# Reordered stage ends, joined score matmuls and narrow value matmuls in a two-layer decoder trunk

## The chip, the cores and the metric

The kernel runs on one core of a Trainium2 chip. The metric is the device time of one execution in microseconds (us), median over runs. A core has a matrix engine (PE, whose weight loads are shown as PEld), a vector engine (DVE), an activation engine (ACT), a general engine (POOL) and a queue that starts transfers (SP). They run side by side and wait for one another on semaphores; each works through its own instructions in the order in which they are written.

## What is computed

Two layers over 512 tokens of 1024 features. Layer 0 mixes tokens by differential attention, layer 1 by native sparse attention (NSA); both go on with a gated MLP and a gated per-layer embedding:

```python
hn = rms_norm(x, g0); a = mixer(hn); x = x + rms_norm(a, g1)
hn = rms_norm(x, g2); f = conv_ffn(hn); x = x + rms_norm(f, g3)
gate = sigmoid(rms_norm(x, ple_g) @ gate_w); x = x + gate * (p[i] @ proj_w)
# differential attention, 8 heads: two score maps, their softmaxes p0 and p1
a = p[:, :, 0] - lam * p[:, :, 1]; o = a @ v; o = rms_norm(o, subln_g); out = o @ w_out
# NSA, 4 groups of 4 heads: three branches, gated
s_c = q @ k_cmp; p_c = masked_softmax(s_c); o_c = p_c @ v_cmp   # compressed keys and values
o = o_c * gates[..., 0] + o_s * gates[..., 1] + o_w * gates[..., 2]; out = o @ w_out
```

With 512 tokens the selected and the window branch both see every earlier key.

## The kernel before

All projections read their weights as *units* of 128x1024 numbers, in one fixed order (PLAN). SP loads a unit into one of four raw buffers, ACT copies it as the high part w_hi (`w_high`), and POOL forms the low part w_lo in four pieces (`low`). PE multiplies three times for each product: high by high, high by low, low by high. `weights(u)` on PE waits until the low parts of all units before u are done. Activations are split in the same way: PE transposes a tile, ACT copies it as nT_hi, DVE subtracts and writes nT_lo. Eight PSUM banks are named A[0..3] and B[0..3]. The order of the work on each engine is written by hand, as one long program an engine.

*Start.* For each of four token tiles: statistics (ACT), xn (DVE), transposes (PE), nT_hi, nT_lo, then the matmuls of the first two units v on that tile.

*Differential heads.* `head(h, ...)` takes four query tiles qt in turn: scores in B, maxima (DVE), two exponentials (ACT), the mix (DVE, amix), transposes into A[2] (`turn_mix`), their copy pT (ACT, `p_turned`), values into A[3]. The head before is normalised at the same time: ACT squares, DVE sums, POOL takes the inverse root by Newton steps and writes o_nrm, PE turns it into A[2] (`turn_o`), ACT and DVE split it (`oT_high`, `oT_low`). The last head has no next head's projections to fill PE; it has parts of the output projection (`early`, units 24 to 26) instead. The output projection's first unit is 27 (PLAN["out0"]).

*Embedding step.* `embed` ends layer 0; its last tile overlaps with the norms for layer 1, in which ACT switches between sigmoid and root.

*NSA groups.* `group(g, first)` projects two query units, the keys and the values, ropes them (DVE), makes the compressed scores (L1651), then takes 16 steps (h, k), in which k stands for query tile ORDER[k] = 0, 3, 1, 2 and n = (tile + 1) * 128 keys. A step has two branches c: scores in B[2 * (k % 2) + c], maxima, two exponentials into gp, transposes into A[2] and A[3] (`gturn`), copies gpT (ACT for c = 0, DVE for c = 1), and values into A[c] (`gvalues`). PE's order in the loop is gturn(n), scores(n+2), values(n-1). Before the loop stand the turning of the compressed weights pc (`cturn`, into A[3], copied as pcT), the turning of the values (`vturn`, into A[0], copied as Vg), and the compressed values (`cvalues(0)`, `cvalues(1)`, read by DVE's `blocks_out`).

The matmul of the values reads 128 columns though only 64 of them are read later:

```python
m = pe.matmul(A[c][:, tok(qt)], gpT[:, k % 2, c, kb * P:(kb + 1) * P],
              Vg[:, kb, HEAD * c:HEAD * c + P], start=kb == 0, stop=kb == qt)
```

## Time and profile before

| | before |
|---|---|
| median of 3 runs | 1501.54 us (1501.36 to 1501.85) |
| profiled execution | 1501.17 us, span 1499.4 us |
| PE busy, share of the span | 97% |
| PE weight loads | 81% |
| DVE, ACT, POOL | 48%, 48%, 46% |
| mean granted clock of PE | 0.998 |
| moved by DMA | 127.80 MB, 85 GB/s |

The span goes from the first to the last instruction. In a timeline row the first number is the start, the second the length of the instruction or of the merged run (xN instructions of one kind). A length of a matmul includes its way through the array, so matmuls start more closely than their lengths say. A bracket shows how long the engine stood idle before the row and what released it. fp32r operands make one matmul record, plain f32 operands two.

### The profile page before, as it was taken

What the parts mean: (1) busy time and instruction counts of PE and PEld (TensorE: products, weight loads), DVE (VectorE), ACT (ScalarE), POOL (GpSimd) and SP (SyncE); (2) the same over time, 40 slices, a digit from 0 to 9 for tenths busy, and PEclk for the clock granted to TensorE, in tenths of its full rate; (3) what the DMA queues carried; (4) which work ended last, traced back from release to release, by engine and by line L of the source; (5) the groups of instructions that cost most, each with busy time, mean ns of one, the idle gap of its engine ahead of it and who ended that gap; (6) DMA issues with size and microseconds to landing.
All of it is one profiled execution on the core that took longest, in us unless ns stands there. A gap on an engine that the chain in (4) does not pass through costs nothing.

```text
span 1499.4 us, 23490 instructions
## 1 busy us (share of the span) xinstructions
PE 1461.4 (97%) x7566; PEld 1215.3 (81%) x7566; DVE 722.3 (48%) x1257; ACT 713.4 (48%) x1298; POOL 688.3 (46%) x982
## 2 busy tenths in 40 slices
PE   6999999999999999999999999999999999999998
PEld 5877768888888888878878888888888888888887
DVE  5477773643434300345476767673544443410053
ACT  5245555644444413456464646464554444423262
POOL 4634446665655655363420211112466565655452
PEclk9999999999999999999999999999999999999999
DMA  6321113323232322242310101001232323232221
GB/s 212 115 71 57 56 43 113 118 97 107 84 100 96 100 96 98 69 159 95 128 57 16 43 15 42 28 28 37 87 116 98 98 87 107 86 111 93 92 98 57
DMA packets 38139, 127.80 MB, mean 85 GB/s; under 512 B 6208, under 2 KB 6976, under 8 KB 37824
## 3 DMA queue, kind: packets, MB, share of 16 engines
q1 hardware_dynamic: 32832, 117.46, 23.4%
q10 hardware_dynamic: 5248, 9.55, 1.8%
q8 instruction: 37, 0.61, 0.2%
q14 instruction: 22, 0.18, 0.0%
HBM read 124.90 MB, written 2.10 MB: 85 GB/s over the span
## 4 chain that ended last, share of the span: by engine, by line
PE 40%; issue 34%; POOL 21%; DVE 2%; ACT 2%; POOLq 0%; ACTq 0%; DVEq 0%
POOL w_lo L304 21%; PE banks_a L1282 21%; PE banks_a L1292 8%; PE banks_b L1292 7%; PE banks_b L1466 1%; PE banks_a L1485 1%; PE banks_a L1255 1%; PE banks_b L1469 0%; ACT y L371 0%; ACT w_hi L368 0%; PE banks_b L1255 0%; DVE nm L1004 0%; DVE xn L832 0%; ACT pT L625 0%; DVE amix L1017 0%
## 5 line engine op out<-in xcount | busy, mean ns | idle before, releaser
L304 POOL TENSOR_TENSOR w_lo<-w_raw,w_hi 128x256 fp32r<-128x256 f32 x864 | 658.7, 795 | 750.6 <-ACT w_hi L368 750.3
L368 ACT ACTIVATE w_hi<-w_raw 128x1024 fp32r<-128x1024 f32 x216 | 228.9, 1062 | 267.9 <-PE banks_b L1292 115.0
L1282 PE MATMUL banks_a<-nT_hi,w_hi 128*128 128x512 f32 (+1 forms) x968 | 344.3, 377 | 0.0
L1282 PE MATMUL banks_a<-nT_lo,w_hi 128*128 128x512 f32 (+1 forms) x968 | 343.2, 376 | 0.7 <-DVE nT_lo L838 0.7
L1282 PE MATMUL banks_a<-nT_hi,w_lo 128*128 128x512 f32 (+1 forms) x968 | 342.1, 375 | 1.1 <-POOL w_lo L304 1.0
L1282 PEld LDWEIGHTS banks_a<-nT_hi,w_lo 128*128 128x128 f32 x968 | 173.5, 189 | 33.8 <-POOL w_lo L304 1.5
L1282 PEld LDWEIGHTS banks_a<-nT_lo,w_hi 128*128 128x128 f32 x968 | 173.8, 189 | 31.9 <-DVE nT_lo L838 0.9
L1282 PEld LDWEIGHTS banks_a<-nT_hi,w_hi 128*128 128x128 f32 x968 | 173.7, 189 | 31.9 <-ACT nT_hi L401 0.3
L910 DVE SCALAR_TENSOR_TENSOR y<-banks_a,conv,y 128x511 f32<-128x511 f32 x88 | 66.0, 750 | 217.7 <-ACT y L494 217.2
L494 ACT ACTIVATE y<-banks_a,conv 128x512 f32<-128x512 f32 x88 | 68.6, 780 | 206.6 <-PE banks_a L1282 206.5
L1004 DVE TENSOR_REDUCE nm<-banks_b 128x2 f32<-128x256 f32 (+2 forms) x96 | 79.2, 825 | 22.6 <-PE banks_b L1469 10.3
L741 ACT ACTIVATE gp<-banks_b,nm 128x128 f32<-128x128 f32 (+3 forms) x128 | 67.6, 528 | 44.4 <-DVE nm L1004 38.7
L1719 PE MATMUL banks_a<-Vg,gpT 128*128 128x128 f32 x640 | 84.6, 280 | 0.0
L1719 PEld LDWEIGHTS banks_a<-Vg,gpT 128*128 128x128 f32 x640 | 76.5, 192 | 0.3
L849 DVE TENSOR_TENSOR y<-banks_b,g_post 128x512 f32<-128x512 f32 x16 | 11.1, 692 | 131.9 <-ACT y L371 131.9
L912 DVE SCALAR_TENSOR_TENSOR y<-banks_a,conv,y 128x510 f32<-128x510 f32 x88 | 65.9, 749 | 12.1
L1292 PE MATMUL banks_a<-w_hi,hT_hi 128*128 128x512 f32 x176 | 69.1, 392 | 0.0
L1292 PE MATMUL banks_a<-w_hi,hT_lo 128*128 128x512 f32 x176 | 68.5, 389 | 0.0
L1292 PE MATMUL banks_a<-w_lo,hT_hi 128*128 128x512 f32 x176 | 68.5, 389 | 0.0
L1292 PE MATMUL banks_b<-w_hi,hT_hi 128*128 128x512 f32 x176 | 68.5, 389 | 0.0
L1292 PE MATMUL banks_b<-w_lo,hT_hi 128*128 128x512 f32 x176 | 68.5, 389 | 0.0
L1292 PE MATMUL banks_b<-w_hi,hT_lo 128*128 128x512 f32 x176 | 68.5, 389 | 0.0
(262 smaller groups left out, 2386.8 us busy)
## 6 DMA issues: line engine op xcount, KB each, us to landing
w_raw<-in_w SPq DMA_DIRECT2D x216, 512.0 KB, 3.3
g_pre<-in_gains ACTq DMA_DIRECT2D x6, 512.0 KB, 4.6
x<-in_x SPq DMA_DIRECT2D x4, 512.0 KB, 8.4
g_post<-in_gains ACTq DMA_DIRECT2D x4, 512.0 KB, 5.7
out<-x SPq DMA_DIRECT2D x8, 256.0 KB, 2.0
pe_raw<-in_pT ACTq DMA_DIRECT2D x2, 512.0 KB, 6.0
w1k<-in_w ACTq DMA_DIRECT2D x1, 1024.0 KB, 5.7
w1v<-in_w ACTq DMA_DIRECT2D x1, 1024.0 KB, 7.8
```

The source lines that it names most:

```text
L304: pool.tensor_tensor(w_lo[slot][:, cols], w_raw[k % RAW][:, cols], w_hi[slot][:, cols].bitcast(F32), ALU.subtract).then_inc(S["w_lo_done"], 1)
L368: act.activation(w_hi[u % RING][:, :], w_raw[u % RAW][:, :], ACT.Copy).then_inc(S["w_hi_done"], 1)
L494: signal(act.activation(dst, bank[:, :], ACT.Identity, bias=conv[:, bass.ds(4 * f + 3, 1)], scale=conv[:, bass.ds(4 * f + 2, 1)]), "aff_do ...
L741: signal(act.activation(gp[:, k % 2, c, 0:n], B[2 * (k % 2) + c][:, 0:n], ACT.Exp, bias=nm[:, qt, c:c + 1], accum_out=sums[:, h % 2, qt, c ...
L910: link(dve.scalar_tensor_tensor(dst[:, 1:SEQ], bank[:, 0:SEQ - 1], conv[:, bass.ds(4 * f + 1, 1)], dst[:, 1:SEQ], ALU.mult, ALU.add))
L912: last = dve.scalar_tensor_tensor(dst[:, 2:SEQ], bank[:, 0:SEQ - 2], conv[:, bass.ds(4 * f, 1)], dst[:, 2:SEQ], ALU.mult, ALU.add)
L1004: signal(dve.tensor_reduce(nm[:, qt, :], banks_b[:, b:b + 2, 0:n], AX.X, ALU.max, negate=True), negmax, step + 1)
L1255: return pe.matmul(dst, src, ident[:, :], start=True, stop=True, is_transpose=True)
L1282: m = pe.matmul(bank[:, cols], w[:, k * P:(k + 1) * P], r[:, k, cols], start=(k, pas) == (0, 0), stop=(k, pas) == (KT - 1, 2))
L1292: m = pe.matmul(bank[:, :], a[:, kk, tok(t)], w[:, c * HALF:(c + 1) * HALF], start=(kk, pas) == (first, 0), stop=(kk, pas) == (last, 2))
L1466: pe.matmul(B[2 * (qt % 2) + c][:, 0:n], qT[p][rows, tok(qt)], kT[p][rows, 0:n], start=True, stop=False)
L1719: m = pe.matmul(A[c][:, tok(qt)], gpT[:, k % 2, c, kb * P:(kb + 1) * P], Vg[:, kb, HEAD * c:HEAD * c + P], start=kb == 0, stop=kb == qt)
```

## The change

1. Start: PE waits for unit v+1's low part before its second unit and not before its first; on ACT the copies of units 2 and 3 stand ahead of nT_hi of tiles 2 and 3.
2. Last differential head: the early part of tile 1, unit 26, moves ahead of turn_mix(2); unit 27's matmuls on tile 0 (`first_output`) fill the places behind the turnings; turn_o of head 6 goes to B[1]; values(2) comes before turn_mix(3).
3. Embedding step: the copy of unit Ub+5 stands ahead of the last sigmoid.
4. Group 0: the subtraction for kc's low part and a memset move ahead of DVE's work on the first queries; the exp table is asked for earlier.
5. All groups: cturn goes to A[1]; the first exponentials stand ahead of the copy pcT; one Vg copy and not two; the second exponentials stand ahead of the first gpT copy; both compressed values come behind the first turning; DVE takes the second maxima ahead of the compressed sums.
6. Scores of both branches lie in one bank for n <= 256 and are made by joined matmuls.
7. Value matmuls read 64 columns.

```diff
--- before.py
+++ after.py
@@ -203,7 +203,7 @@
             ("cm", [P, 2, TT * N_PAD], F32),
-            ("Vg", [P, TT, P + HEAD], F32), ("vT", [P, SEQ], F32),
+            ("Vg", [P, TT, P], F32), ("vT", [P, SEQ], F32),
@@ -248,6 +248,17 @@
             return cols.rearrange("p (n j o) -> p o j n", j=CMP_STRIDE // 2, o=2)[:, odd, :, :]
+        def score_columns(k):
+            n, b = (ORDER[k] + 1) * P, 2 * (k % 2)
+            if n <= 2 * P:
+                return banks_b[:, b, 0:2 * n].rearrange("p (c n) -> p c n", c=2)
+            return banks_b[:, b:b + 2, 0:n]
+        def turned_o(h):
+            return B[1] if isinstance(h, int) and h == DIFF_HEADS - 2 else A[2]
@@ -556,9 +567,9 @@
                 link(square(x[:, 2, HALF:D], ss[:, 1, 2:3], y0[:, 2, :]))
+                w_high(Ub + 5)
                 second(3)
                 root(q, 2)
-                w_high(Ub + 5)
                 stats(q, 3)
@@ -578,10 +589,10 @@
             input_stats(3)
+            w_high(2)
+            w_high(3)
             nT_high(0, 2)
             nT_high(0, 3)
-            w_high(2)
-            w_high(3)
             act.wait_ge(S["consts_ready"], 5)
...
@@ -773,23 +784,23 @@
                            8 * g + 6 + c + 1)
+                if first:
+                    act.activation(std[:, TT:TT + 1], eps[:, :], ACT.Exp)
                 act.wait_ge(S["cexp_in"], g + 1)
                 signal(act.activation(vT[:, :], A[2], ACT.Copy), "vT_done", g + 1)
+                gexps(*seq[0])
                 act.wait_ge(S["cpT_done"], g + 1)
-                signal(act.activation(pcT[:, :, :], A[3].rearrange("p (t n) -> p t n", t=TT), ACT.Copy),
+                signal(act.activation(pcT[:, :, :], A[1].rearrange("p (t n) -> p t n", t=TT), ACT.Copy),
                        "cpTc_done", g + 1)
-                gexps(*seq[0])
                 act.wait_ge(S["vTt_done"], g + 1)
                 v3 = A[0].rearrange("p (t n) -> p t n", t=TT)
-                link(act.activation(Vg[:, :, 0:P], v3, ACT.Copy))
-                signal(act.activation(Vg[:, :, P:P + HEAD], v3[:, :, 0:HEAD], ACT.Copy), "vg_done", g + 1)
+                signal(act.activation(Vg[:, :, :], v3, ACT.Copy), "vg_done", g + 1)
+                gexps(*seq[1])
                 for n, (h, k) in enumerate(seq):
                     gp_turned(h, k)
-                    if n == 0:
-                        gexps(*seq[1])
                     if n == 3:
@@ -797,7 +808,7 @@
             group(0, True, u=UG)
-            with chain.loop(1, GROUPS, 1) as g:
+            with chain.loop(1, GROUPS, 0) as g:
                 group(g, False, i=g, u=UG, per=4)
@@ -997,12 +1008,13 @@
-            def maxima(qt, b, scores, negmax, step):
+            def maxima(qt, b, scores, negmax, step, columns=None):
                 dve.wait_ge(S[scores], 2 * step + 2)
-                signal(dve.tensor_reduce(nm[:, qt, :], banks_b[:, b:b + 2, 0:n], AX.X, ALU.max, negate=True), negmax,
-                       step + 1)
+                if columns is None:
+                    columns = banks_b[:, b:b + 2, 0:n]
+                signal(dve.tensor_reduce(nm[:, qt, :], columns, AX.X, ALU.max, negate=True), negmax, step + 1)
...
@@ -1155,6 +1167,11 @@
                             goT_low(2 * g - 2 + m, m)
+                    if n == 0 and first:
+                        dve.wait_ge(S["kchi_done"], 1)
+                        dve.tensor_tensor(kc[:, :, 1, :], kcmp[:, :, :], kc[:, :, 0, :].bitcast(F32), ALU.subtract)\
+                            .then_inc(S["kclo_done"], 1)
+                        dve.memset(Kl[side(1), :, :].bitcast(F32), 0.0)
                     if n < 2:
@@ -1163,10 +1180,6 @@
                     if n == 1 and first:
-                        dve.wait_ge(S["kchi_done"], 1)
-                        dve.memset(Kl[side(1), :, :].bitcast(F32), 0.0)
-                        dve.tensor_tensor(kc[:, :, 1, :], kcmp[:, :, :], kc[:, :, 0, :].bitcast(F32), ALU.subtract)\
-                            .then_inc(S["kclo_done"], 1)
                         dve.wait_ge(S["cm_in"], 16)
@@ -1195,6 +1208,7 @@
                     .then_inc(S["cp_done"], 1)
+                gmaxima(*seq[1])
                 dve.wait_ge(S["cp_done"], g + 1)
...
@@ -1217,9 +1230,10 @@
-                blocks_out(0)
                 for n, (h, k) in enumerate(seq):
                     gp_turned(h, k)
+                    if n == 0:
+                        blocks_out(0)
                     if n + 2 < len(seq):
@@ -1428,9 +1442,9 @@
                     pe.wait_ge(S["nlo_done"], 2 * t)
-                    if t == 1:
-                        weights(PLAN["v"] + 2)
                     for n in range(2):
+                        if t == 1:
+                            weights(PLAN["v"] + n + 1)
                         m = of_tiles(PLAN["v"], n, (t - 1,), A, nT_hi, nT_lo, KT)
@@ -1489,7 +1503,7 @@
                 for t in range(TT):
-                    m = transpose(A[2][:, tok(t)], o_nrm[:, t, :])
+                    m = transpose(turned_o(h)[:, tok(t)], o_nrm[:, t, :])
                 m.then_inc(S["oT_done"], 1)
@@ -1523,8 +1537,10 @@
                         early(0, *(n for n in parts if n < 2))
-                    elif parts[0]:
-                        early(1, 2)
+                def first_output(c):
+                    weights(PLAN["out0"] + 1)
+                    tokens(B[0], PLAN["out0"] % RING, c, oT0_hi, oT0_lo, c, 0, KT)
                 pe.wait_ge(S["qrope_done"], h + 1)
@@ -1539,7 +1555,17 @@
                     later_part(h + 2, p, 0, 4)
+                if not keys:
+                    early(1, 2)
                 turn_mix(h, 2)
+                if not keys:
+                    first_output(0)
+                    turn_o(h - 1)
+                    values(h, 2)
+                    turn_mix(h, 3)
+                    first_output(1)
+                    values(h, 3)
+                    return
                 later_queries(0)
@@ -1570,7 +1596,9 @@
             U = PLAN["out0"]
-            by_unit(U, range(3), B, oT0_hi, oT0_lo, KT, last_head)
+            pe.wait_ge(S["oTlo_done"], DIFF_HEADS - 1)
+            of_tiles(U, 0, (1, 2, 3), B, oT0_hi, oT0_lo, KT).then_inc(S["units_done"], 1)
+            by_unit(U, range(1, 3), B, oT0_hi, oT0_lo, KT, last_head)
             last_of_first(U, 3, B, oT0_hi, oT0_lo, KT, last_head)
@@ -1657,7 +1685,7 @@
                     for t in range(TT):
-                        m = transpose(A[3][:, tok(t)], pc[:, t, :, :].rearrange("p h n -> p (h n)"))
+                        m = transpose(A[1][:, tok(t)], pc[:, t, :, :].rearrange("p h n -> p (h n)"))
                     m.then_inc(S["cpT_done"], 1)
@@ -1685,13 +1713,21 @@
                         pe.wait_ge(S["gprobs_done"], 2 * step(h, k) - 2)
+                    both = score_columns(k)
+                    if n <= 2 * P:
+                        for K in (Kh, Kl):
+                            pe.matmul(both, Q[h][:, tok(qt)], K[:, :, 0:n], start=K is Kh, stop=False)
+                        pe.matmul(both[:, :, n - P:n], ident_b[:, :],
+                                  causal_b[:, :].unsqueeze(1).broadcast_to([P, 2, P]), start=False,
+                                  stop=True).then_inc(S["gscores_done"], 2)
+                        return
                     for c in range(2):
                         for K in (Kh, Kl):
-                            pe.matmul(B[2 * (k % 2) + c][:, 0:n], Q[h][:, tok(qt)], K[:, c, 0:n],
-                                      start=K is Kh, stop=False)
+                            pe.matmul(both[:, c, :], Q[h][:, tok(qt)], K[:, c, 0:n], start=K is Kh, stop=False)
                     for c in range(2):
-                        pe.matmul(B[2 * (k % 2) + c][:, n - P:n], ident_b[:, :], causal_b[:, :], start=False,
+                        pe.matmul(both[:, c, n - P:n], ident_b[:, :], causal_b[:, :], start=False,
                                   stop=True).then_inc(S["gscores_done"], 1)
@@ -1716,8 +1752,8 @@
                         for kb in range(qt + 1):
-                            m = pe.matmul(A[c][:, tok(qt)], gpT[:, k % 2, c, kb * P:(kb + 1) * P],
-                                          Vg[:, kb, HEAD * c:HEAD * c + P], start=kb == 0, stop=kb == qt)
+                            m = pe.matmul(A[c][:, qt * P:qt * P + HEAD], gpT[:, k % 2, c, kb * P:(kb + 1) * P],
+                                          Vg[:, kb, side(c)], start=kb == 0, stop=kb == qt)
                     m.then_inc(S["gpv_done"], 1)
@@ -1743,7 +1779,6 @@
                 vturn()
-                cvalues(0)
                 for n, (h, k) in enumerate(seq):
@@ -1751,6 +1786,7 @@
                     else:
+                        cvalues(0)
                         cvalues(1)
```

## Rows read from the trace of the kernel before

**Rows 1.** Page of the profile, first part: busy time, share, instructions.

```profile
PE 1461.4 (97%) x7566; PEld 1215.3 (81%) x7566; DVE 722.3 (48%) x1257; ACT 713.4 (48%) x1298; POOL 688.3 (46%) x982
```

**Rows 2.** Who waited for whom, PE: total us, times, longest us.

```profile
PE banks_a L1255 <- ACT gp L741: 3.9, 4, 1.0
```

**Rows 3.** Timeline at the start: start us, us, instruction, [idle before it <- releaser].

```profile
13.49 1.40 DVE L838 TENSOR_TENSOR nT_lo<-banks_a,nT_hi 128x512 fp32r<-128x512 f32 x2
...
17.02 0.76 PE L1292 MATMUL banks_a<-w_hi,nT_hi 128*128 128x512 f32 x1 [2.28 <-POOL w_lo L304]
...
21.64 1.04 PE L1255 MATMUL banks_b<-ident,xn 128*128 128x128 f32 x8
...
22.33 1.23 ACT L401 ACTIVATE nT_hi<-banks_b 128x512 fp32r<-128x512 f32 x2 [4.63 <-PE banks_b L1255]
```

**Rows 4.** Busy time by stretch, and the granted clock (after POOL's figures).

```profile
225.00:229.00 4.00, 3.79 (x14) 3.13 (x15) 1.48 (x2) 0.85 (x2) 0.00 (x0) 0.59 0.00 0
...
757.50:761.50 4.00, 4.00 (x14) 3.21 (x14) 3.83 (x8) 2.10 (x4) 0.92 (x2) 0.58 0.37 131
```

**Rows 5.** Timeline of the last differential head and of its output projection.

```profile
224.03 0.55 PE L1255 MATMUL banks_a<-ident,amix 128*128 128x128 f32 x3 [1.19 <-DVE amix L1017]
225.21 0.71 PE L1255 MATMUL banks_a<-ident,o_nrm 128*128 128x128 f32 x4 [0.63 <-ACT pT L625]
...
230.93 0.47 PE L1292 MATMUL banks_b<-w_hi,oT_hi 128*128 128x512 f32 x1
...
241.95 0.60 PE L1255 MATMUL banks_a<-ident,o_nrm 128*128 128x128 f32 x4
...
230.00 2.01 ACT L368 ACTIVATE w_hi<-w_raw 128x1024 fp32r<-128x1024 f32 x2
...
240.49 1.04 POOL L333 TENSOR_TENSOR o_nrm<-o_raw,osum 128x512 f32<-128x512 f32 x1
```

**Rows 6.** Timeline of the change from layer 0's embedding step to layer 1.

```profile
695.79 0.60 ACT L526 ACTIVATE sg<-banks_b 128x512 f32<-128x512 f32 x1 [1.05 <-issue]
...
698.02 1.06 ACT L368 ACTIVATE w_hi<-w_raw 128x1024 fp32r<-128x1024 f32 x1
...
703.35 1.22 PE L1282 MATMUL banks_a<-nT_hi,w_lo 128*128 128x256 f32 x8 [1.00 <-POOL w_lo L304]
```

**Rows 7.** Timeline of the entry into group 0.

```profile
747.85 1.42 DVE L1162 TENSOR_TENSOR Q<-banks_b,Q 64x512 fp32r<-64x512 f32 x2 [2.73 <-ACT Q L758]
...
754.54 0.91 DVE L1167 MEMSET Kl<- 64x1024 f32 x1 [0.27 <-DVE Q L1162]
...
755.90 1.94 PE L1651 MATMUL banks_a<-kc,Q 128*128 128x64 f32 x16 [1.66 <-DVE kc L1168]
...
764.07 1.28 ACT L777 ACT_TABLE_LOAD   x1 [2.23 <-DVE sc L1190]
...
766.84 0.66 PE L1255 MATMUL banks_a<-ident,pc 128*128 128x128 f32 x4 [0.18 <-DVE pc L1196]
```

**Rows 8.** Timeline of the first turnings of group 2.

```profile
909.64 0.66 PE L1255 MATMUL banks_a<-ident,pc 128*128 128x128 f32 x4
...
915.48 1.09 PE L1255 MATMUL banks_a<-ident,gp 128*128 128x128 f32 x8 [1.04 <-ACT gp L741]
```

**Rows 9.** Timeline of PE's small matmuls in group 2.

```profile
918.11 0.30 PE L1691 MATMUL banks_b<-Kh,Q 128*128 128x128 f32 x1
...
918.72 2.00 PE L1719 MATMUL banks_a<-Vg,gpT 128*128 128x128 f32 x16
920.56 0.82 PE L1255 MATMUL banks_a<-ident,gp 128*128 128x128 f32 x6
...
923.35 0.36 PE L1691 MATMUL banks_b<-Kh,Q 128*128 128x256 f32 x1
923.55 0.28 PE L1691 MATMUL banks_b<-Kl,Q 128*128 128x256 f32 x1
...
900.27 1.97 PE L1651 MATMUL banks_a<-kc,Q 128*128 x16
```

More of the change, by code:

```diff
@@ L637, in oT_high @@
                 act.wait_ge(S["oT_done"], h + 1)
-                signal(act.activation(oT0_hi[:, bass.ds(h, 1), :].rearrange("p a n -> p (a n)"), A[2][:, :],
+                signal(act.activation(oT0_hi[:, bass.ds(h, 1), :].rearrange("p a n -> p (a n)"), turned_o(h),
                                       ACT.Identity, scale=subg[:, :]), "oThi_done", h + 1)
@@ L740, in gexps @@
                             act.wait_ge(S["gT_done"], 2 * step(h, k) - 2)
-                        signal(act.activation(gp[:, k % 2, c, 0:n], B[2 * (k % 2) + c][:, 0:n], ACT.Exp,
+                        signal(act.activation(gp[:, k % 2, c, 0:n], score_columns(k)[:, c, :], ACT.Exp,
                                               bias=nm[:, qt, c:c + 1],
@@ L1037, in oT_low @@
                 signal(dve.scalar_tensor_tensor(
-                    oT0_lo[:, bass.ds(h, 1), :].rearrange("p a n -> p (a n)"), A[2][:, :], subg[:, :],
+                    oT0_lo[:, bass.ds(h, 1), :].rearrange("p a n -> p (a n)"), turned_o(h), subg[:, :],
                     oT0_hi[:, bass.ds(h, 1), :].rearrange("p a n -> p (a n)").bitcast(F32), ALU.mult, ALU.subtract),
@@ L1122, in gmaxima @@
                 def gmaxima(h, k):
-                    maxima(ORDER[k], 2 * (k % 2), "gscores_done", "gnegmax_done", step(h, k))
+                    maxima(ORDER[k], 2 * (k % 2), "gscores_done", "gnegmax_done", step(h, k), score_columns(k))
                 def gp_turned(h, k):
```

1 line of the change is left out of this document (removed).

## The prediction, made before the changed kernel was run

> **What bounds the kernel now.** I read the page of the profile first, then who waited for whom, then the timeline at each place the diff touches, then the busy time by stretch. The page says that one engine sets the time: PE is busy for 97% of the span, the others for under half [rows 1]. So only two things can gain: PE work that goes away, and places where PE stands still. In the waits, note how small they are: the largest repeated one is 3.9 us in four pieces of at most 1.0 [rows 2]. The rest sit at the ends of stages, each with its releaser: 2.28 us at the start [rows 3], 1.19 and 0.63 in the last differential head [rows 5], 1.00 before layer 1 [rows 6], 1.66 at the entry of group 0 [rows 7], and about 1 in each group [rows 8]. Two of these cost more than their length: right behind them the granted clock is 0.59 and 0.58 for 4 us, that is, half of it at the 1.2 GHz level [rows 4], some 1.6 us lost each time, for a pause of under 2 us.
>
> **The change part by part.** The sum is made against the profiled execution's own 1501.17 us (span 1499.4); the median of the three runs is 1501.54, so 0.4 more.
>
> *Start.* PE waited for the low parts of units 0 and 1; now only unit 0's hold back the first matmul, and what comes last is nT_lo, done at 13.49 + 1.40 = 14.89 [rows 3]. The first matmul moves from 17.02 to 15.0: gain 2.0. Unit 1's low parts are done before PE has finished its six matmuls of unit 0, since they were ready at 17.0. The twelve matmuls of the first tile took 21.64 - 17.02 = 4.62 us, against 48 in 241.95 - 230.93 = 11.02, or 0.23 each, later on [rows 3, 5]: they are mostly at the lower clock. If the full clock comes back at the same moment as before, 1.0 of the 2.0 is lost again; if the unbroken work brings it sooner, 0.9 is added. Bounds 1.0 to 2.9. Two weight copies (1.06 us each) now stand on ACT ahead of nT_hi of tile 2; ACT was idle for 4.63 us there [rows 3], so 2.1 us is covered even with the tile 2 us earlier. Without that cover it would cost up to 1 us.
>
> The Trainium skill (TensorE: Matmul & The Clock Gate, section on the HAM clock gate) says that the clock's decision runs on its own time and doesn't start with the kernel. By it the start gives 1.0 or 2.9 and seldom 2.0; this trace shows only one phase and can't say which.
>
> *Last head.* The stretch from the start of the first wait (224.03 - 1.19 = 222.84) to the first output matmul took 230.93 - 222.84 = 8.09 us [rows 5]. Its work at full rate is six 512-column matmuls (1.47), eleven transposes (1.3) and fourteen value matmuls (1.8), 4.6 in all. Now six matmuls of unit 27 and the moved early part fill the waits for amix and pT, and the turned output of head 6 goes to B[1], so it needn't wait until pT has been copied out of A[2]. That gives 8.1 - 4.6 = 3.5, less 0.1 for restarts: 3.4. What is late next is the last head's own o_nrm: the POOL chain ends 240.49 + 1.04 = 241.53, 11.5 us after the weight copies at 230.00, and these follow the last p_turned, which moves up by only 2.3, to 227.7. So o_nrm is ready at 239.3, and PE comes to it at 241.95 - 3.4 = 238.55 [rows 5]: a new wait of about 0.8. Net 2.6; bounds 1.0 (the chain doesn't move up, except by the first wait) and 3.8.
>
> *Before layer 1.* The copy of unit Ub+5 (1.06 us at 698.02) moves into ACT's pause of 1.05 ahead of the sigmoid [rows 6]. Its low parts start 3 us earlier, so PE's 1.00 wait goes; root and xn slip by 0.05. Net 0.95, bounds 0.3 and 1.0.
>
> *Entry of group 0.* The kc subtraction moves ahead of the queries, and with it the 0.91 memset [rows 7]; DVE stood idle for 2.73 us there, for ACT's first query copies [rows 7], which covers both (uncovered: 1.2). The compressed scores start at 754.35 instead of 755.90, and the half-clock stretch behind the pause [rows 4] should go. Next late is the key chain: rope, Kh and its copies end 1.4 earlier, at about 760.5, and the first scores wait 0.5 for it. The exp table (1.28) is loaded in ACT's idle 2.23 [rows 7] and not behind the scores. Following both chains I get the turning of pc at 764.1 instead of 766.84: 2.7, of which 0.2 is counted under scores below. With 0.3 from the new order behind it: 2.8. Bounds 1.5 (only the wait goes) and 3.6.
>
> *Groups 1 to 3, order.* From cturn to the second turning is 915.48 - 909.64 = 5.84 us [rows 8]. Now the first exponentials don't wait for the compressed copy, the second follow the values copy directly, and the compressed values fill PE. The second turning then needs ACT's vT, two exponentials, two copies, two exponentials and gpT, which ends at 913.8: 1.7 earlier. DVE gives some back. The second step's maxima now come before its 2 us of compressed sums, but these stand ahead of the first gpT copy, blocks_out(0) and the third maxima, which end at 914.9. Behind them ACT copies the second gpT until 916.95, so PE waits 0.8 at the third turning. Net 0.7 a group, 2.1 for three; bounds 0 (all given back) and 5.0 (nothing).
>
> *Joined scores.* A k=0 step is six matmuls, 918.72 - 918.11 = 0.61 us. Joined it is one 256-column matmul behind transposes (923.55 - 923.35 = 0.20), one more (0.12) and one causal (0.12): 0.44 [rows 9]. 0.17 for 16 steps is 2.7. A k=2 step has two 512-column matmuls for four of 256 and comes out even. Bounds 1.4 (each joined matmul 0.2) and 4.3 (each 0.113).
>
> *Narrow values.* 640 matmul records go from 128 to 64 columns. Sixteen of 128 columns take (2.00 - 0.28) / 15 = 0.115 us each, 0.28 being the last one's own length; sixteen of 64 columns, with the same 128 weights, take (1.97 - 0.28) / 15 = 0.113 [rows 9]. So the weight load sets the pace, not the columns: 640 x 0.002 = 1.3 at most. I take 0.6; bounds 0 and 1.3. The second Vg copy on ACT is off the path from then on.
>
> The Trainium skill gives two prices (same page). Its table under Back-to-back issue gap lets up to 64 columns go in about 60 cycles instead of 134; its LDWEIGHTS section has 128 weight columns cost 107 ns however short the matmul. The second agrees with the 0.113 row; the first would be the rival below.
>
> Sum: 2.0 + 2.6 + 0.95 + 2.8 + 2.1 + 2.7 + 0.6 = 13.75. 1501.17 - 13.75 = 1487.4, and by the median 1487.8: I say 1487.6.
>
> **Rivals.** *The waits only move* (0.15). DVE's and ACT's chains or POOL's o_nrm eat what the orders free. With every low bound the gain is 1.0 + 1.0 + 0.3 + 1.5 + 0 + 1.4 + 0 = 5.2, 1496; half-way to the forecast is 1492. For it: I find two new waits myself, and DVE and ACT work between PE's steps all through a group. Against: most edits move work into idle time that a row shows.
>
> *Narrow values run narrow* (0.05). If a 64-column record took 0.06, 40 records a head would save 2.2 us; 16 heads 35. About half of them lie between a long step's scores and its own turning, where PE already waits for ACT, and would turn into waiting: 17 us more, 1470. Against: the 0.113 row.
>
> *Joined operands read slowly* (0.03), the one that ends slower. The joined matmuls read K in two runs of 128 or 256 columns. At a third of the rate a k=0 step takes 0.96 and a k=2 step 1.6, 1.27 us more a head, 20 for sixteen: 1501.2 - 11.05 + 20 = 1510. It decides from 0.9 us a head on. Nothing like that shows in the runs of the compression matmuls, whose operand has gaps too.
>
> The Trainium skill (SBUF — State Buffer, under Door 1: The DMA port swizzle) says that a non-contiguous PSUM pattern slows matmuls much; here only the joined causal matmul of k=2 writes in two runs, and no row of before shows such a write.
>
> *Nothing measurable* (0.03): only if new pauses bring the half clock back at several places, 1.6 us each.
>
> **Chances.** The forecast has 0.74, with its own range 1483 to 1491.5; with the first rival 0.89. The range takes in the first rival's nearer half and an earlier clock: 1482 to 1494. Within 0.2% is within 3 us, about what this measurement can tell from no change. Faster 0.93, same 0.04, slower 0.03.
>
> **What would show it.** In the changed kernel's timeline: first matmul near 15.0; a wait of about 0.8 before o_nrm of the last head, and granted clock 1.0 there and at the entry of group 0; no POOL wait before layer 1; 0.44 us for a k=0 step; value records still near 0.113; a new wait at each group's third turning. I am wrong if value records fall to 0.06, if joined steps are longer than 0.61, or if the o_nrm wait exceeds 2 us.

## The result, and the profile after

The changed kernel took 1486.91 us (median of five runs, 1486.11 to 1487.17) against 1501.70 for the kernel before (1501.36 to 1501.92). The ratio is 0.9901, with a 95% interval from 0.9887 to 0.9916: faster by 14.8 us. The profiled execution took 1487.17, with a span of 1485.4 against 1499.4, and it is this difference of 14.0 that is followed below.

The page's first part, where [rows 1] showed 1461.4 us of busy PE in 97% of the span:

```profile
PE 1451.7 (98%) x7470; PEld 1202.9 (81%) x7470; DVE 721.1 (49%) x1257; ACT 711.5 (48%) x1295; POOL 687.4 (46%) x982
```

PE has 9.7 us less to do, in 96 fewer instructions, and stands still for some 4 us less. Its waits, by who released it (total us, times, longest us), where [rows 2] stood:

```profile
PE banks_a L1269 <- ACT gp L752: 7.0, 16, 0.7
...
PE banks_a L1269 <- POOL o_nrm L344: 0.9, 1, 0.9
```

The wait for ACT's exponentials has grown, from 3.9 us in 4 pieces to 7.0 in 16. Fifteen of the 16 stand at a k=1 turning, one in each head of the groups but one, and this row becomes the key to the larger errors below. The ends of the stages, on the timeline (start, us, instruction, idle before it and releaser), where [rows 3, 5, 6] showed 17.02, 21.64, 240.49 and the wait of 1.00:

```profile
15.02 0.80 PE L1306 MATMUL banks_a<-w_hi,nT_hi 128*128 128x512 f32 x1 [0.21 <-DVE nT_lo L849]
...
19.46 1.03 PE L1269 MATMUL banks_b<-ident,xn 128*128 128x128 f32 x8
...
237.11 0.63 PE L1269 MATMUL banks_a<-ident,o_nrm 128*128 128x128 f32 x4 [0.91 <-POOL o_nrm L344]
...
226.59 5.62 POOL L315 TENSOR_TENSOR w_lo<-w_raw,w_hi 128x256 fp32r<-128x256 f32 x8 [3.79 <-ACT w_hi L379]
...
235.92 1.04 POOL L344 TENSOR_TENSOR o_nrm<-o_raw,osum 128x512 f32<-128x512 f32 x1
...
655.74 0.47 PE L1306 MATMUL banks_b<-w_hi,pe_hi 128*128 128x512 f32 x1 [0.45 <-POOL w_lo L315]
...
695.43 1.23 PE L1269 MATMUL banks_b<-ident,xn 128*128 128x128 f32 x8 [0.85 <-DVE xn L843]
```

The first matmul is at 15.02, and its wait is now for nT_lo. The o_nrm wait foretold at 0.8 is there with 0.91, and POOL's eight pieces of w_lo (5.62 us) stand ahead of the chain that makes o_nrm. Before layer 1 no wait for POOL is left, only one for xn that was 0.65 and is 0.85. The wait at 655.74 is new. The clock, by stretch (it is the third figure from the end), in the last head and behind the compressed scores, where [rows 4] had 0.59 and 0.58:

```profile
225.00:229.00 4.00, 3.96 (x21) 3.08 (x21) 0.59 (x2) 3.90 (x6) 2.40 (x4) 1.00 0.00 0
749.00:753.00 4.00, 4.00 (x26) 3.46 (x26) 3.79 (x9) 1.75 (x3) 2.58 (x4) 1.00 0.40 133
```

The entry of group 0 and the group after it, where [rows 7] had the compressed scores at 755.90 and the turning of pc at 766.84:

```profile
740.12 0.29 DVE L1172 TENSOR_TENSOR kc<-kcmp,kc 128x128 fp32r<-128x128 f32 x1
...
749.20 1.97 PE L1679 MATMUL banks_a<-kc,Q 128*128 128x64 f32 x16
...
754.84 1.28 ACT L788 ACT_TABLE_LOAD   x1
...
758.49 0.66 PE L1269 MATMUL banks_a<-ident,pc 128*128 128x128 f32 x4
```

The first turnings of group 2, and then one value matmul of each later step, where [rows 8, 9] stood:

```profile
898.34 0.66 PE L1269 MATMUL banks_a<-ident,pc 128*128 128x128 f32 x4 [0.22 <-DVE pc L1209]
...
902.95 1.06 PE L1269 MATMUL banks_a<-ident,gp 128*128 128x128 f32 x8 [0.71 <-ACT gp L752]
...
905.33 0.63 PE L1269 MATMUL banks_a<-ident,gp 128*128 128x128 f32 x4
905.71 0.36 PE L1720 MATMUL banks_b<-Kh,Q 128*128 128x256 f32 x1
...
906.15 1.90 PE L1755 MATMUL banks_a<-Vg,gpT 128*128 128x64 f32 x16
907.96 0.85 PE L1269 MATMUL banks_a<-ident,gp 128*128 128x128 f32 x6
...
913.24 1.06 PE L1269 MATMUL banks_a<-ident,gp 128*128 128x128 f32 x8 [0.38 <-ACT gp L752]
...
916.22 1.90 PE L1755 MATMUL banks_a<-Vg,gpT 128*128 128x64 f32 x16
918.20 0.85 PE L1269 MATMUL banks_a<-ident,gp 128*128 128x128 f32 x6
...
923.47 0.74 PE L1269 MATMUL banks_a<-ident,gp 128*128 128x128 f32 x5 [0.38 <-ACT gp L752]
```

From the turning of pc to the second turning it is 902.95 - 898.34 = 4.61 us, before 5.84. A k=0 step takes 906.15 - 905.71 = 0.44, before 0.61. Sixteen value records take (1.90 - 0.28) / 15 = 0.108 each, before 0.115. And a head, from its k=1 turning to the next, takes 923.47 - 913.24 = 10.23 us, with a wait of 0.38. A smaller wait has no bracket: from the sixteen value records to the k=3 turning behind them it is 907.96 - 906.15 = 1.81 us in the first head and 918.20 - 916.22 = 1.98 in the next, 0.17 more for the same matmuls.

Between landmarks that both traces have, the 14.0 us come from these stretches (they sum to 14.05; tile 2 is the third of the four token tiles, and the end of group 3 is the end of its last value matmul):

| stretch | predicted | measured |
|---|---|---|
| start, to the transposes of tile 2 | 2.0 | 21.64 - 19.46 = 2.18 |
| on to the last o_nrm turning | 2.6 | 4.84 - 2.18 = 2.66 |
| on to the first transposes of layer 1 (685.56 and 681.57) | 0 | -0.85 |
| on to the second layer of the compression (742.12 and 737.08) | 0.95 | 1.05 |
| on to group 0's turning of pc (0.2 of the scores in it) | 2.7 | 3.31 |
| on to the end of group 3 (0.3 + 2.1 + 2.5 + 0.6) | 5.5 | 5.70 |

### The profile page after: what moved, and what is told of

Read it like the earlier page. It is cut to its first block, busy times and chain, and to the rows that moved or that the text cites. A ratio compares the mean times of both kernels' runs of the same rounds, so it can differ in the third digit from the quotient of the medians.

```text
span 1485.4 us, 23294 instructions
## 1 busy us (share of the span) xinstructions
PE 1451.7 (98%) x7470; PEld 1202.9 (81%) x7470; DVE 721.1 (49%) x1257; ACT 711.5 (48%) x1295; POOL 687.4 (46%) x982
## 4 chain that ended last, share of the span: by engine, by line
PE 41%; issue 33%; POOL 21%; DVE 2%; ACT 2%; DMA 1%; POOLq 0%; SPq 0%; ACTq 0%; DVEq 0%
PE banks_a L1296 21%; POOL w_lo L315 21%; PE banks_a L1306 8%; PE banks_b L1306 7%; PE banks_b L1480 2%; PE banks_a L1499 1%; PE banks_a L1269 1%; DMA x<-in_x 1%; ACT y L382 0%; PE banks_b L1483 0%; DVE xn L843 0%; PE banks_b L1269 0%; ACT w_hi L379 0%; ACT pT L636 0%; DVE nm L1017 0%
## 5 line engine op out<-in xcount | busy, mean ns | idle before, releaser
L1755 PE MATMUL banks_a<-Vg,gpT 128*128 128x64 f32 x640 | 80.2, 272 | 0.0
```

The costliest lines, as they stand in the source:

```text
L1755: m = pe.matmul(A[c][:, qt * P:qt * P + HEAD], gpT[:, k % 2, c, kb * P:(kb + 1) * P], Vg[:, kb, side(c)], start=kb == 0, stop=kb == qt)
```

## The experiments

Beside the times, each kernel is read at these landmarks, since one matmul start can be compared to within 0.1 us inside a stage, while the median of a few runs is uncertain by 1 to 2 us.

**The ends alone.** The kernel before, with points 1 to 3 of the change: start, last head and embedding step. The entry edit of group 0, which the expectation names, was left out of this kernel by mistake; it has its own run further down.

```diff
+            w_high(2)
+            w_high(3)
             nT_high(0, 2)
...
+                if not keys:
+                    first_output(0)
+                    turn_o(h - 1)
...
+                w_high(Ub + 5)
                 second(3)
```

> The kernel before with the edits at the start, in the last differential head, in the embedding step and at the entry of group 0 alone; nothing inside the groups. If each stage end adds its own gain (2.15 + 2.7 + 1.0 + 3.1 us in the profiles of before and after), this gives about 8.2 to 9 us: some 1493. If the half-clock stretches are chance and not tied to the waits, it gives 3 us less, 1496.

Measured: 1496.69 us (1493.99 to 1498.38) against 1502.18, ratio 0.9963 (0.9949 to 0.9977). The stretches repeat those of the change: 1.91 at the start, 2.76 in the last head, 1.07 before the compression. What the missing edit left is instructive:

```profile
750.13 1.94 PE L1669 MATMUL banks_a<-kc,Q 128*128 128x64 f32 x16 [1.66 <-DVE kc L1172]
...
761.07 0.66 PE L1259 MATMUL banks_a<-ident,pc 128*128 128x128 f32 x4 [1.23 <-DVE pc L1200]
...
752.00:756.00 4.00, 3.81 (x17) 2.81 (x16) 3.80 (x9) 2.38 (x4) 0.64 (x1) 1.00 0.42 131
```

Here the wait of 1.66 before the compressed scores is followed by a granted clock of 1.00, not 0.58 as in [rows 4], and yet the stretch from those scores to the turning of pc is 761.07 - 750.13 = 10.94 us, to the hundredth what it was before (766.84 - 755.90). PE only stands longer in front of that turning, 1.23 us for DVE. So the half clock there cost nothing: the chain of DVE and ACT set the end of the stretch. Three more kernels have the same wait, two with the half clock behind it (joined scores and the new order, 10.96 and 10.93 us) and one without it (narrow values, 10.94).

**Joined scores alone.**

```diff
+                        for K in (Kh, Kl):
+                            pe.matmul(both, Q[h][:, tok(qt)], K[:, :, 0:n], start=K is Kh, stop=False)
```

> The kernel before with joined score matmuls alone. By my reading of the rows 0.17 us for each of 16 steps with k = 0 and nothing for k = 2: 2.7 us less, 1499. If both kinds of step gain: 4 to 5 us less. If the joined read of K in two runs is slow: no gain or a loss.

Measured: 1500.79 (1499.18 to 1501.71) against 1502.18, ratio 0.9993 (0.9983 to 1.0003): no difference. From the turning of pc in group 0 to the end of group 3 it took 258.43 us, before 259.14, so 0.7 at most came through, where 2.7 was expected. The k=1 turnings:

```profile
926.27 1.06 PE L1263 MATMUL banks_a<-ident,gp 128*128 128x128 f32 x8 [0.28 <-issue]
...
936.50 1.07 PE L1263 MATMUL banks_a<-ident,gp 128*128 128x128 f32 x8 [0.27 <-issue]
```

The same two in the kernel before:

```profile
925.80 1.06 PE L1255 MATMUL banks_a<-ident,gp 128*128 128x128 f32 x8 [0.22 <-issue]
...
936.08 1.06 PE L1255 MATMUL banks_a<-ident,gp 128*128 128x128 f32 x8 [0.22 <-issue]
```

A head takes 936.50 - 926.27 = 10.23 us, and in the kernel before 936.08 - 925.80 = 10.28. Of the 0.17 us that the k=0 step gives up, 0.05 is left in the period: the step got shorter and PE came no sooner to the next k=1 turning.

**Narrow values alone.**

```diff
-                            m = pe.matmul(A[c][:, tok(qt)], gpT[:, k % 2, c, kb * P:(kb + 1) * P],
-                                          Vg[:, kb, HEAD * c:HEAD * c + P], start=kb == 0, stop=kb == qt)
+                            m = pe.matmul(A[c][:, qt * P:qt * P + HEAD], gpT[:, k % 2, c, kb * P:(kb + 1) * P],
+                                          Vg[:, kb, side(c)], start=kb == 0, stop=kb == qt)
```

> The kernel before with 64-column value matmuls and one Vg copy alone. If the weight load sets the pace, 0.6 us less (0 to 1.3), 1501. If the columns do, over 10 us less.

Measured: 1499.38 (1498.41 to 1501.43), ratio 0.9983 (0.9974 to 0.9993); the stretch of the groups 256.37, so 2.8 us shorter. That is more than the 0 to 1.3 expected and far from the 10 of the rival.

```profile
913.72 1.09 PE L1254 MATMUL banks_a<-ident,gp 128*128 128x128 f32 x8 [0.84 <-ACT gp L741]
...
923.97 1.06 PE L1254 MATMUL banks_a<-ident,gp 128*128 128x128 f32 x8 [0.32 <-issue]
```

A head takes 10.24 us again (923.97 - 913.72 is 10.25), although its forty value records save 0.3. But the second turning comes 913.72 - 908.38 = 5.34 us after that of pc, and before 5.84: 0.50, and with 0.42 to 0.70 in the other groups 2.1 in all. This is the second copy of Vg, 0.38 us and its restart on ACT, which stood ahead of the second exponentials. No value matmul stands between these two turnings, so the narrower columns have no part in this; the copy that they made needless has it.

**The new order alone.** Point 5 without the single Vg copy.

```diff
+                gexps(*seq[1])
                 for n, (h, k) in enumerate(seq):
                     gp_turned(h, k)
-                    if n == 0:
-                        gexps(*seq[1])
```

> The kernel before with the new order at the head of each group alone. I expect 0.7 us in each of groups 1 to 3 and 0.2 in group 0, 2.3 in all, 1499.3, with a new wait of about 0.8 at the third turning. If nothing is given back behind the second turning, it is 1.7 a group, 6 to 7 us in all.

Measured: 1497.81 (1496.47 to 1499.46), ratio 0.9972 (0.9962 to 0.9982); the stretch of the groups 255.66, 3.5 us shorter.

```profile
911.68 1.06 PE L1255 MATMUL banks_a<-ident,gp 128*128 128x128 f32 x8 [1.06 <-ACT gpT L751]
...
921.97 1.06 PE L1255 MATMUL banks_a<-ident,gp 128*128 128x128 f32 x8 [0.22 <-issue]
```

The second turning follows that of pc (906.65) by 5.03 us, 0.81 sooner than before, the third by 7.27, 0.84 sooner than before: the wait of 0.8 that was expected there did not come. A head takes 10.29, as before, since nothing in it was changed.

**The kc subtraction late again.** The changed kernel, with kc's low part and the memset back behind the second queries.

```diff
                     if n == 1 and first:
+                        dve.wait_ge(S["kchi_done"], 1)
+                        dve.memset(Kl[side(1), :, :].bitcast(F32), 0.0)
+                        dve.tensor_tensor(kc[:, :, 1, :], kcmp[:, :, :], kc[:, :, 0, :].bitcast(F32), ALU.subtract)\
+                            .then_inc(S["kclo_done"], 1)
```

> The changed kernel with DVE's kc subtraction and memset put back behind the second query unit. If the wait for kc brings back the half clock, the loss is the 1.5 us wait plus about 1.6 us less what the key chain hides: 2.5 to 3.3 us more than the changed kernel, with a granted clock near 0.6 behind the wait. If the half clock came only by chance, 1.5 us more at most and the clock stays at 1.0.

Measured: 1489.61 (1488.17 to 1491.2) against 1501.17, ratio 0.9924 (0.9907 to 0.9940). The wait of 1.66 is back, the clock stays at 1.00 behind it, and from the second hidden layer to the turning of pc it takes 23.39 us and not 21.41: 1.98 us for this edit, without any half clock. The clock is as the second theory had it, the cost above its bound of 1.5.

**Values of 16 columns.** The question was whether the columns or the weights set the pace of the value records.

```diff
-                            m = pe.matmul(A[c][:, qt * P:qt * P + HEAD], gpT[:, k % 2, c, kb * P:(kb + 1) * P],
-                                          Vg[:, kb, side(c)], start=kb == 0, stop=kb == qt)
+                            m = pe.matmul(A[c][:, qt * P:qt * P + 16], gpT[:, k % 2, c, kb * P:(kb + 1) * P],
+                                          Vg[:, kb, HEAD * c:HEAD * c + 16], start=kb == 0, stop=kb == qt)
```

> The changed kernel with value matmuls of 16 columns in place of 64; it leaves out 48 of the 64 columns of each head's selected and window outputs. If the 128-column weight load sets the pace, a value record stays at 0.11 us and the time within 0.5 us of the changed kernel. If columns count, a record falls to 0.06 or less and the time by several us.

Measured: 1496.51 (1492.42 to 1498.65), ratio 0.9963 (0.9950 to 0.9977), so 9.6 us slower than the changed kernel by the medians and 8.7 in the profiled executions, with a mean clock of 0.993 (0.991 to 0.995 in its seven runs, 0.999 to 1.000 in the five of the changed kernel). One run of values, and the granted clock in three stretches:

```profile
911.63 1.86 PE L1755 MATMUL banks_a<-Vg,gpT 128*128 128x16 f32 x16
...
797.00:805.00 8.00, 7.54 (x36) 6.57 (x36) 2.80 (x8) 0.90 (x3) 0.00 (x0) 0.69 0.00 1
869.00:877.00 8.00, 7.52 (x43) 7.26 (x43) 3.25 (x10) 2.22 (x6) 0.00 (x0) 0.67 0.01 2
944.00:949.00 5.00, 4.85 (x30) 4.53 (x31) 2.30 (x7) 0.53 (x2) 0.00 (x0) 0.78 0.00 0
```

Sixteen records of 16 columns take 1.86 us, of 64 columns 1.90, of 128 columns 2.00: the columns do not set the pace, and the rival of narrow records is out. That the load of 128 weight columns sets it is what is left, but no run here changes the weights. A head keeps its 10.23 us where the clock is full. The loss is the clock. It fell to half four times, once toward the end of each group (the first three are shown), where the changed kernel has 1.00 throughout.

**Only k=0 joined.** The changed kernel with the k=2 scores in four matmuls of 256 columns again.

```diff
-            if n <= 2 * P:
+            if n <= P:
```

> The changed kernel with scores joined only for k = 0; k = 2 goes back to four matmuls of 256 columns in two banks. My reading is that joining k = 2 is even: within 0.5 us of the changed kernel. If joining k = 2 carries part of the gain, up to 1 to 2 us slower.

Measured: 1487.21 (1485.24 to 1487.59), ratio 0.9906 (0.9889 to 0.9922): as the changed kernel. A k=2 step takes 0.69 us so (909.50 - 908.81) and 0.67 joined (911.41 - 910.74 in the changed kernel). Joined operands are not read slowly, nor does the causal matmul's write in two runs cost anything.

**The entry of group 0 alone.** What the first run left out, on the kernel before.

```diff
+                if first:
+                    act.activation(std[:, TT:TT + 1], eps[:, :], ACT.Exp)
                 act.wait_ge(S["cexp_in"], g + 1)
...
+                    if n == 0 and first:
+                        dve.wait_ge(S["kchi_done"], 1)
+                        dve.tensor_tensor(kc[:, :, 1, :], kcmp[:, :, :], kc[:, :, 0, :].bitcast(F32), ALU.subtract)\
```

> The kernel before with the edits at the entry of group 0 alone (the subtraction of kc and its memset ahead of the first queries, the exponential's table loaded before the scores), which the first experiment left out. My theory: both rows of the stretch shorten, the wait of 1.66 us before the compressed scores and the table load behind them; from the end of the second hidden layer to the turning of pc it was 24.7 us, and in the changed kernel 21.4, of which 0.3 to 0.8 belongs to the joined scores and the new order. So 2.5 us less here: 1499.2. Rival: the other parts of the change carry it (in the changed kernel with the late kc 1.98 us came back, so the table alone would be worth 1.3 there), and alone the edit gives under 1.5: above 1500.2. If the half clock behind the wait cost anything, a further 1 us goes when it does not appear.

Measured: 1498.24 (1496.86 to 1499.32) against 1501.52, ratio 0.9977 (0.9967 to 0.9986).

```profile
755.27 1.97 PE L1654 MATMUL banks_a<-kc,Q 128*128 128x64 f32 x16
...
764.55 0.66 PE L1258 MATMUL banks_a<-ident,pc 128*128 128x128 f32 x4
```

From the second hidden layer (743.16) to the turning of pc it takes 21.39 us, in the changed kernel 21.41, before 24.72. So the edit alone carries all 3.3 us; neither the joined scores nor the new order have a share in this stretch. Of the 3.3, 1.98 came back with the late kc, so about 1.3 is left for the table load.

**Split maxima.** From here on the kernels go beyond the change, to attack what it left: the 0.38 us in each head.

```diff
+                    if k == 1:
+                        for c in range(2):
+                            signal(dve.tensor_reduce(nm[:, qt, c:c + 1], banks_b[:, b + c, :], AX.X, ALU.max,
```

> The changed kernel, with the maxima of each head's 512-column step (k=1) taken in two instructions of 512 columns, the first signalled on its own, so that ACT's first exponential starts while DVE still reduces the second half. In the changed kernel PE waits 0.38 us for ACT at this step's turning in each head, and a head takes 10.23 us: the chain is scores, maxima of 1.23, two exponentials of 0.88, turning. Theory: that chain is what the joined scores' and the narrow values' savings ran into. With the split the first exponential starts 0.54 us earlier, the 0.38 goes, and a head takes about 9.87: 13 to 15 heads by 0.36 are 5 us, 1481.9. Rival: PE's wait is only one of several equal chains (DVE's copies of gpT, ACT's order), and the wait comes back at the next turning: within 1.5 us of the changed kernel, 1485.5 or more.

Measured: 1484.84 (1483.29 to 1486.37) against 1501.52, ratio 0.9883 (0.9867 to 0.9900).

```profile
930.25 1.42 DVE L1142 TENSOR_REDUCE nm<-banks_b 128x1 f32<-128x512 f32 x2 [0.43 <-PE banks_b L1741]
...
931.06 0.69 ACT L755 ACTIVATE gp<-banks_b,nm 128x512 f32<-128x512 f32 x1 [1.18 <-DVE nm L1142]
...
933.20 1.07 PE L1280 MATMUL banks_a<-ident,gp 128*128 128x128 f32 x8
```

The wait at the k=1 turning is gone, and a head takes 933.20 - 923.19 = 10.01 us, the one before it 10.07. That is half of what was expected, and the time lies between the theory's 1481.9 and the rival's 1485.5: the chain is confirmed, but not as the only one. In the groups the gain was 2.0 us, from 253.44 to 251.43. In this execution pe_raw landed late and PE waited 1.48 us for w_lo at the embedding step, which the next but one run takes up.

**Scores first.**

```diff
+                    if ahead:
+                        gscores(*seq[n + 2])
                     gturn(h, k)
```

> The changed kernel, with the scores of step n+2 issued ahead of the turning of step n on PE, and DVE's maxima of it ahead of its copy of gpT, for the steps k=3 and k=0 of each head. It attacks the same wait of 0.38 us from the other side: the 512-column scores start 0.6 us earlier. Theory (the chain runs through DVE too): DVE's copy of the k=3 step's gpT now stands behind the 1.23 us of maxima, so that PE waits some 0.5 us for it at the next turning, and a head stays at 10.1 to 10.4 us: 1484 to 1489. Rival (only PE's order counts): the 0.38 goes and nothing comes back, 1482 or less.

Measured: 1482.49 (1482.44 to 1483.85), ratio 0.9874 (0.9858 to 0.9891). A head takes 9.92 us, 0.3 less, better than I expected, and a new wait stands at the k=1 turning:

```profile
928.48 0.69 DVE L1017 TENSOR_REDUCE nm<-banks_b 128x2 f32<-128x512 f32 x1
929.21 0.29 DVE L1140 COPY gpT<-banks_a 128x128 f32<-128x128 f32 x1
...
929.65 0.96 PE L1272 MATMUL banks_a<-ident,gp 128*128 128x128 f32 x7 [0.22 <-DVE gpT L1140]
```

The wait that I expected, for the copy of the k=3 step, did not come: the k=2 scores now lie ahead of the k=0 turning and cover that copy. What is late is the k=0 copy, at 929.21, behind the k=2 maxima on DVE. PE's order and DVE's needn't be the same.

**Copies into idle time.**

```diff
+                if not keys:
+                    w_high(PLAN["early0"] + RING)
                 exps(h, p, 2)
...
+                w_high(Ua + RING)
+                w_high(Ua + 1 + RING)
                 act.wait_ge(S["ple_in"], 16 * (layer + 1))
```

> The changed kernel with two of ACT's weight copies moved into its idle time, at two places far apart. In the last differential head the first of two copies moves ahead of the third exponentials (ACT idle 1.13 us there), so that POOL makes its low part 3.8 us earlier and the o_nrm chain is not held up behind eight of POOL's pieces. Theory: the wait of 0.91 us at the turning of o_nrm is POOL's queue; o_nrm is ready at about 235, PE comes at 236.2, the wait goes: 0.9 us. At the embedding two copies move ahead of ACT's wait for pe_raw (idle 10.9 us): the wait of 0.45 us for w_lo goes where pe_raw lands late. Together 0.9 to 1.4: 1485.5 to 1486. Rival: o_nrm is held by its own chain (DVE's sums, thirteen small steps on POOL), which starts at ACT's copy of o_raw: then 0.5 us or more of the wait stays.

Measured: 1483.97 (1483.46 to 1484.31), ratio 0.9881 (0.9865 to 0.9898), about 2.9 us faster than the changed kernel in its own runs and 3.4 in the profiled executions, more than the 0.9 to 1.4 expected.

```profile
222.25 2.81 POOL L315 TENSOR_TENSOR w_lo<-w_raw,w_hi 128x256 fp32r<-128x256 f32 x4
...
233.21 1.04 POOL L344 TENSOR_TENSOR o_nrm<-o_raw,osum 128x512 f32<-128x512 f32 x1
...
235.53 0.60 PE L1270 MATMUL banks_a<-ident,o_nrm 128*128 128x128 f32 x4
```

POOL makes the first low part from 222.25 on, o_nrm starts at 233.21 and is ready at 234.25, and PE turns it at 235.53 without a wait. From the transposes of tile 2 to that turning it takes 216.43 us and not 217.65: 1.2. At the embedding step the wait for w_lo is gone too: from V's turning to the first pe matmul it takes 396.79 us, not 397.47. Here pe_raw landed as late as in the changed kernel, 413.5 us after the turning of o_nrm against 413.4, and PE did not wait. But four other variants of the changed kernel (late kc, 16 columns, k=0 joined, scores first) reach the pe matmul without a wait and without this edit, since pe_raw landed sooner; so this 0.7 is had only in executions in which it lands late. Behind it two more waits of PE, 0.43 and 0.19 in the changed kernel, are gone: from the first pe matmul to the first transposes of layer 1 it takes 24.80 us, and not 25.83. It is 24.82 in the next kernel, which has the edit too, and 25.1 to 25.9 in the twelve without it, so this is more than scatter. The start's scatter gives 0.4 of the 3.4.

**All of them.** The two moved copies, PE's scores first for k=3 and k=0, DVE's maxima first for k=3 alone.

```diff
+                    ahead = 0 < n < len(seq) - 2 and k == 3
+                    if ahead:
+                        gmaxima(*seq[n + 2])
                     gp_turned(h, k)
```

> The changed kernel with what the last four runs left over put together: the two weight copies moved as in the run on the head and the embedding; PE's scores ahead of the turning for the steps k=3 and k=0; and DVE's maxima ahead of its copy of gpT for k=3 alone. In the run with both steps moved on DVE too, a head took 9.92 us and PE waited 0.22 us for DVE's copy of the k=0 step's gpT, which stood behind the k=2 maxima of 0.69. Theory: with that copy first again the 0.22 goes, 12 to 16 heads by 0.22 are 2.6 to 3.5 us, and the o_nrm wait of 0.9 and up to 0.5 at the embedding go as before: 1482.5 less 4 is 1478.5. A head takes 9.7 us and PE waits only at the heads of the groups. Rival: the second exponentials of k=2 are now late in its place (their maxima end 0.3 us later), the turning of k=2 waits, and only the 1.0 to 1.4 of the other two edits come: 1481 to 1481.5.

Measured: 1478.44 us (1478.07 to 1478.74, five runs) against 1501.10, ratio 0.9848 (0.9835 to 0.9861). This beats both kernels: 22.7 us faster than the one before, 8.5 faster than the changed one.

```profile
916.50 1.04 PE L1273 MATMUL banks_a<-ident,gp 128*128 128x128 f32 x8
...
926.10 1.04 PE L1273 MATMUL banks_a<-ident,gp 128*128 128x128 f32 x8
```

A head now takes 926.10 - 916.50 = 9.60 us in place of 10.28, with no wait at the k=1 turning. An estimate of PE's own work in a head gives the same: 10.28 of before, less its wait of 0.22, less 0.17 for the joined k=0 step and 0.28 for forty value records (0.007 each), is 9.61. So next to nothing of the 9.60 is still a wait.

## Why the prediction was right, and which terms were off

The sum was 13.75 us and the span shortened by 14.0. The steps one by one:

- *Start.* As predicted: the first matmul at 15.02 for 15.0. The full clock comes at another moment in each execution. The granted clock reads 1.00 all through this stretch, so the moment is read from the matmuls: their starts go from 0.43 us apart to 0.23 at 19.78 to 23.32 in the five traces with the old start, and at 17.53 to 20.98 in the nine with the new one. So the transposes of tile 2 scatter by 1.0 to 1.3 us between kernels with the same start (20.94 to 22.22 in the five, 18.91 to 19.88 in the nine). The difference of the means is 2.4 us, within the bounds 1.0 to 2.9.
- *Last head.* 2.66 for 2.6, and its new wait 0.91 for 0.8, on the instruction that was named. The half clock behind the old pauses (a granted clock of 0.57 to 0.77 from 226 to 230 in five traces without the edit) is 1.00 in all nine with it. (The prediction calls 0.59 "half of it at the 1.2 GHz level". A mean of 0.59 between 0.5 and 1 is four fifths of the stretch at the lower level, and the 1.6 us lost follow from that.)
- *Before layer 1.* 1.05 for 0.95. Ahead of it 0.6 us were lost where nothing had been changed: pe_raw landed 0.9 us later after its issue, and w_lo with it. The run with the moved copies shows that the weight copies in ACT's queue stood behind that transfer: with pe_raw as late, 413.5 us after the turning of o_nrm against 413.4, PE didn't wait. Where pe_raw landed sooner (412.1 in the kernel with k=0 joined, 412.5 before) nothing was lost.
- *Entry of group 0.* 3.31 for 2.7. The step that failed is "the first scores wait 0.5" for the key chain. The prediction doesn't write it out, but I had taken DVE's step on cm, which stands ahead of the rope, at its 0.75 us of before. It took 0.23, so the rope came earlier and nothing waited. The half clock, which [rows 4] show at 0.58 and which was to go, cost nothing, as the first run shows.
- *Groups.* 5.70 for 5.5, but by errors that cancel. *Joined scores* were sized at 2.7 and brought 0.7 at most alone. *Narrow values* were sized at 0.6 and brought 2.8, of which 2.1 is the second Vg copy. That copy's place ahead of the second exponentials was in the code, and I had counted it as "off the path from then on". The price of a record was off too: 0.115 to 0.108 saves 0.007 and not 0.002, over 640 records 4.5 us and not "1.3 at most", and most of that went into waits. *The order* was sized at 2.4, group 0's 0.3 included, and brought 3.5; the predicted wait of 0.8 at the third turning wasn't there. (Two kernels that do the same in this stretch differ by 0.45 in it, so each share may be 0.4 less.) Together they give 5.7 and not the 7.0 of their sum, for the most part because joined scores and narrow values both run into one floor, whose 0.05 a head can be had only once.

That the total came within 0.25 us is therefore partly luck: 0.85 us lost where nothing was changed, 0.6 more than forecast gained at the entry of group 0, and three terms of the groups that were off by 2.0, 2.2 and 1.1 us, with different signs.

That floor is the step which I didn't take. The prediction counted PE work that goes away in full, because PE is busy for 97% of the span. But a head of the groups was bound by a loop through three engines: the k=3 turning, the k=1 scores, DVE's maxima (1.23 us), ACT's two exponentials (0.88 each), the k=1 turning, DVE's copy, the k=3 maxima and exponentials. PE waits at both turnings, 0.38 and 0.17 us, in the changed kernel. Its sign in the profile of before was the row of 0.22 us, "issue", at each k=1 turning, and the head of 10.28 lay only 0.05 us above what the loop allows. With joined scores a head takes 10.23 us, with narrow values 10.24, with both 10.23. Two changes of the loop itself, one on DVE and one of PE's order with DVE's, bring 10.01 to 10.07 and 9.92, and the last kernel 9.60, all with the same matmuls. This was shown, not only argued. What remains open is the share of each link in the loop: no run changes ACT's exponentials or the copies alone.

The Trainium skill (TensorE: Matmul & The Clock Gate, section LDWEIGHTS) has the load of weights take its columns divided by 1.2, in ns, with no term for the matmul's own columns, which gives an estimate of 107 ns for 128. The 0.108 of 64 columns and the (1.86 - 0.28) / 15 = 0.105 of 16 agree. Its table in the section Back-to-back issue gap has about 60 cycles for up to 64 columns, and is given there for an isolated matmul; the records here, each with a weight load of its own, did not go by it. The Trainium skill's warning on non-contiguous PSUM patterns (SBUF — State Buffer, section Door 1: The DMA port swizzle) is not borne out for this one write in two runs of 128 columns: 0.67 us joined, 0.69 in separate matmuls.

## What to carry to other kernels

An engine that is 97% busy can still be paced by a loop through others: take the period of the repeated unit (here one head) and follow which instruction begins at the same distance from which, before pricing work that leaves the busy engine. A small wait that stands once in every period, here one of 0.22 us put down to "issue", can be the mark of such a loop, and shortening what lies outside it then only makes that wait longer. When the scores of a later step are moved ahead on one engine, the engine that serves it may want another order, so move them separately.

## What the runs showed of the hardware that was not expected

- Value matmuls of 16 columns, 0.105 us each and not 0.108, brought the granted clock down to 0.69, 0.67 and 0.78 over the three stretches shown, toward the ends of the groups, and the kernel lost 9.6 us. Less work for PE was not harmless here.
- The half clock behind a pause comes in some executions only. After the same wait of 1.66 us at the entry of group 0 it was there in the kernel before and in the kernels with joined scores and with the new order, and not in the one with the ends, the one with narrow values, and the one with the late kc. Behind the two pauses of the last head, 1.19 and 0.63 us, it was there in all five.
- DVE steps were slower beside POOL's w_lo pieces. The step on cm, 128x128 elements, took 0.75 us in the six traces in which four of these pieces had begun 0.2 us before it, and 0.23 in the eight in which POOL did nothing at that time:

```profile
755.67 0.75 DVE L1171 TENSOR_SCALAR cm<-cm 128x128 f32<-128x128 f32 x1
...
755.46 2.96 POOL L304 TENSOR_TENSOR w_lo<-w_raw,w_hi 128x256 fp32r<-128x256 f32 x4 [2.50 <-ACT w_hi L368]
...
749.18 0.23 DVE L1184 TENSOR_SCALAR cm<-cm 128x128 f32<-128x128 f32 x1
```

  The first two rows are of the kernel before, the third of the changed one. So 0.52 us of what the entry of group 0 gained goes with POOL standing idle there. In the same way four of five small steps on 128x4 elements in the last head took 0.65 to 0.67 us in the changed kernel, beside these pieces, and four of them 0.16 to 0.17 where POOL had finished sooner (the fifth 0.63).
